# A two-layer hybrid decoder trunk: one eviction moved ahead of a softmax normalisation, the last round of transposes on four PSUM banks, the compressed values padded to 128 rows

## The reference

```python
def hybrid_layer(x, g, w_in, ...):
    h = rmsnorm(x, g)
    z = h @ w_in
    u_lru, g_lru, q, g_nsa, kc, vc, ks, vs, kwn, vwn, gate_logits = jnp.split(z, splits, axis=-1)
    y_lru = rg_lru(causal_depthwise_conv(u_lru, conv_w, conv_b), wa, ba, wi, bi, lam)
...
    o_cmp, p_cmp = cmp_attention(q, compress(heads(kc), pos_k, kw1, kw2), compress(heads(vc), pos_v, vw1, vw2))
...
    o_slc = slc_attention(q_rot, apply_rope(heads(ks), cos, sin), heads(vs), idx, ok)
    o_win = win_attention(q_rot, apply_rope(heads(kwn), cos, sin), heads(vwn))
    gates = jax.nn.sigmoid(gate_logits.astype(F32)).reshape(B, S, N_HEADS, 3)
    y_nsa = (gates[..., 0:1] * o_cmp + gates[..., 1:2] * o_slc + gates[..., 2:3] * o_win).reshape(B, S, D_NSA)
    y = jnp.concatenate([y_lru * jax.nn.silu(g_lru), y_nsa * jax.nn.silu(g_nsa)], axis=-1)
    return x + y @ w_out
```

## Time and profile before

| | |
|---|---|
| median of 3 runs | 543.06 us |
| the runs | 539.6, 543.06, 544.32 us |
| time of the profiled execution | 540.08 us |
| its span in the profile | 538.3 us |
| PE busy | 523.8 us, 97% |
| DVE busy | 379.9 us, 71% |
| ACT busy | 309.9 us, 58% |
| mean share of the DMA engines | 40 slices between 1 and 9 tenths, 102 GB/s |

### The profile page before, as it was taken

One profiled execution on the slowest core, in us unless ns is written; L12 is line 12 of the kernel. 1 busy time (PEld: TensorE's weight loads), 2 busy tenths in 40 slices (PEclk: granted clock), 3 DMA queues, 4 the chain that ended last, 5 costly groups with the idle time before them and its releaser, 6 DMA issues.

```text
span 538.3 us, 8590 instructions
## 1 busy us (share of the span) xinstructions
PE 523.8 (97%) x3095; PEld 395.6 (73%) x3095; DVE 379.9 (71%) x620; ACT 309.9 (58%) x625; POOL 46.8 (9%) x88
## 2 busy tenths in 40 slices
PE   8999999999899999999999999999989999999995
PEld 7777868778677766767887687678777777676784
DVE  3596996679857686855747589668986768678432
ACT  5757735624766666663534772653475656667523
POOL 4101100130000000000520110012100000000000
PEclk9999999999999999999999999999999999999999
DMA  9876464365222222321323845635523232111013
GB/s 263 203 226 185 97 180 103 73 149 126 76 74 65 56 55 69 79 58 40 90 90 98 213 124 142 119 94 119 136 62 96 61 97 52 50 38 34 8 41 117
DMA packets 102426, 54.65 MB, mean 102 GB/s; under 512 B 42080, under 2 KB 100592, under 8 KB 102384
## 3 DMA queue, kind: packets, MB, share of 16 engines
q1 hardware_dynamic: 99232, 49.63, 36.1%
q0 software_dynamic: 1536, 3.15, 2.4%
q10 hardware_dynamic: 1616, 1.32, 0.8%
HBM read 44.12 MB, written 2.10 MB: 86 GB/s over the span
## 4 chain that ended last, share of the span: by engine, by line
PE 67%; DVE 16%; issue 5%; SPq 4%; ACT 3%; DMA 3%; POOL 1%; POOLq 0%; DVEq 0%; ACTq 0%
PE z_ps L1634 10%; PE z_ps L1636 10%; PE z_ps L1635 10%; PE o_ps L1775 5%; PE t_ps L1737 5%; PE a_ps L1775 4%; PE s_ps L1714 3%; DVE w_lo L1233 3%; PE z_ps L1714 3%; PE o_ps L1634 3%; PE o_ps L1636 2%; PE o_ps L1635 2%; ACT probs L1160 2%; DMA swp<-E 2%; DVE E L1282 2%
## 5 line engine op out<-in xcount | busy, mean ns | idle before, releaser
L1634 PE MATMUL z_ps<-h_hi,w_hi 128*128 128x512 f32 x248 | 101.5, 409 | 4.3 <-DVE E L1282 4.2
L1636 PE MATMUL z_ps<-h_hi,w_lo 128*128 128x512 f32 x248 | 97.0, 391 | 0.0
L1635 PE MATMUL z_ps<-h_lo,w_hi 128*128 128x512 f32 x248 | 96.8, 390 | 0.0
L982 ACT ACTIVATE w_hi<-stage 128x1024 fp32r<-128x1024 f32 x54 | 57.1, 1058 | 53.9 <-PE z_ps L1636 29.1
L1233 DVE TENSOR_TENSOR w_lo<-stage,w_hi 128x1024 fp32r<-128x1024 f32 x54 | 65.9, 1220 | 8.6 <-ACT w_hi L982 7.9
L1169 ACT ACTIVATE probsT<-t_ps 128x512 f32<-128x512 f32 (+1 forms) x70 | 41.7, 595 | 43.8 <-PE t_ps L1737 34.1
L1634 PEld LDWEIGHTS z_ps<-h_hi,w_hi 128*128 128x128 f32 x248 | 46.6, 188 | 18.7 <-issue 8.2
L1636 PEld LDWEIGHTS z_ps<-h_hi,w_lo 128*128 128x128 f32 x248 | 46.5, 188 | 10.3
L1635 PEld LDWEIGHTS z_ps<-h_lo,w_hi 128*128 128x128 f32 x248 | 46.7, 188 | 8.3 <-issue 0.2
L1522 DVE TENSOR_REDUCE mn<-s_ps 128x1 f32<-128x384 f32 (+3 forms) x44 | 26.2, 637 | 32.4 <-PE s_ps L1722 32.3
L1160 ACT ACTIVATE probs<-s_ps,mn 128x128 f32<-128x128 f32 (+3 forms) x64 | 33.1, 527 | 16.4 <-DVE mn L1522 16.2
(11 more groups left out here) (266 smaller groups left out, 1052.7 us busy)
## 6 DMA issues: line engine op xcount, KB each, us to landing
stage<-in_w_in SPq DMA_DIRECT2D x27, 512.0 KB, 4.1
stage<-in_w_in SPq DMA_DIRECT2D x34, 256.0 KB, 3.9
probsT<-swp SPq DMA_DIRECT2D x72, 64.0 KB, 2.1
stage<-in_cmp_k_w SPq DMA_DIRECT2D x8, 512.0 KB, 4.0
stage<-in_cmp_v_w SPq DMA_DIRECT2D x8, 512.0 KB, 4.5
stage<-in_w_out SPq DMA_DIRECT2D x8, 512.0 KB, 3.3
stage<-in_w_out SPq DMA_DIRECT2D x16, 256.0 KB, 3.7
swp<-E POOLq DMA_DIRECT2D x48, 64.0 KB, 2.3
```

What stands on the lines that cost most here:

```text
L982: act.activation(split_into(n)[0], stage_of(key), ACT.Copy).then_inc(hi_split, 1)
L1634: pe.matmul(bank, w_hi[:, slot, at:at + P], x_hi, start=first, stop=False)
L1635: pe.matmul(bank, w_hi[:, slot, at:at + P], x_lo, start=False, stop=False)
L1636: ins = pe.matmul(bank, w_lo[:, slot, at:at + P], x_hi, start=False, stop=last)
```

## The change

In `attention`, the whole normalisation (now one step `CS2`) moves behind `close()`: DVE evicts gn0 first, and the multiply follows the four small instructions at once. On ACT the order of these steps is unchanged.

The coefficient turn ("B", 3, 1) moves from the end of round 11 to the end of round 12. Since the pieces of a round are spread over its turns, the four pieces of round 11 in layer 1 now stand two and two, and the four of round 12 one behind each turn. The tiles of round 12 use four banks, t_ps1 being the fourth; a turn on it waits for all exponentials of the layer.

vc_sb gets 128 rows, of which POOL zeroes all once at the start of the program, and the compressed tiles are weighed with all 128 rows. ACT still copies 31 rows of a turned compressed tile; the slot's other rows hold what an earlier tile left there and meet zeros.

```diff
@@ attention
     fill(N_START - 2)
-    add(("CS2", 0))
     close()
     split("HI")
-    add(("CS2", 1), *tanhs, *silus)
+    add(*tanhs, ("CS2",), *silus)
     split("LO")
...
-        if n in (1, 2, len(SETS) - 1):
+        if n == len(SETS) - 1:
+            owed, coefs = coefs, []
+        if n == len(SETS):
+            turns += owed
+        if n in (1, 2):
             turns += coefs
             coefs = []
@@ Plan
-            self.turn_bank.append(place[0] % 3 if place else 0)
+            self.turn_bank.append(place[0] if place else 0)
@@ hybrid_trunk
-        kc_bd, vc_sb = sb("kc_bd", [P, N_KV * NC]), sb("vc_sb", [NC, N_KV, HD])
+        kc_bd, vc_sb = sb("kc_bd", [P, N_KV * NC]), sb("vc_sb", [P, N_KV, HD])
...
-        score_banks, turn_banks = [s_ps, [z_ps[1], t_ps[1]]], [t_ps[0], *s_ps]
+        score_banks, turn_banks = [s_ps, [z_ps[1], t_ps[1]]], [t_ps[0], *s_ps, t_ps[1]]
...
-        N_CONST = 7
+        N_CONST = 8
...
-                eng.wait_ge(exp_ok, plan.exps[per_layer(plan.steps, plan.turns[n][0] + 1) - 1])
+                eng.wait_ge(exp_ok, plan.exps[per_layer(plan.steps, plan.turns[n][0] + 1) - (plan.turn_bank[n] < 3)])
...
+            pool.memset(vc_sb[:, :, :], 0.0).then_inc(consts, 1)
...
                 elif kind == "CS2":
-                    _, l, last = st
-                    if last:
-                        dve.tensor_tensor(sc3, sc3, spread(rsc), ALU.mult).then_inc(cs_ok, 1)
-                        continue
+                    l = st[1]
                     dve.wait_ge(cs_exp, l + 1)
...
+                    dve.tensor_tensor(sc3, sc3, spread(rsc), ALU.mult).then_inc(cs_ok, 1)
@@ weigh
                 for g in range(N_KV):
-                    if b < 2:
-                        v, rows = v_sb[:, b, k, g * HD:(g + 1) * HD], P
-                    else:
-                        v, rows = vc_sb[:, g, :], NC
+                    v = v_sb[:, b, k, g * HD:(g + 1) * HD] if b < 2 else vc_sb[:, g, :]
...
-                        turned = slot_of(key)[0:rows, g * 2 * P:(g + 1) * 2 * P]
+                        turned = slot_of(key)[:, g * 2 * P:(g + 1) * 2 * P]
```

More of the change, by code:

```diff
@@ L854, in _ @@
                 kind = st[0]
-                if st == ("CS2", DEPTH - 1, 0):
+                if st == ("CS2", DEPTH - 1):
                     sync.wait_ge(rot_ok, len(plan.rope))
@@ L1461, in _ @@
                     else:
-                        dve.tensor_scalar(vc_sb[:, :, :], bank[0:NC, 0:P].rearrange("p (g d) -> p g d", g=N_KV), 0.5, None,
+                        dve.tensor_scalar(vc_sb[0:NC, :, :], bank[0:NC, 0:P].rearrange("p (g d) -> p g d", g=N_KV), 0.5, None,
                                           ALU.mult).then_inc(a_dve, 1)
```

## The result

| | before | after |
|---|---|---|
| median of 4 runs | 543.35 us (539.6 to 544.32) | 535.08 us (534.57 to 535.71) |
| a second series | 540.98 us (11 runs, 539.94 to 543.22) | 534.64 us (4 runs, 534.44 to 535.18) |
| the profiled execution | 540.08 us, span 538.3 | 534.57 us, span 532.8 |

The ratio is 0.9882, with an interval from 0.9853 to 0.991; in the second series it is 0.9876, from 0.9856 to 0.9896. The changed kernel is 1.2% faster. The two profiled executions stand 5.5 us apart, near the sum of 5.1. But the series stand 6 to 8 us apart in their medians, and the runs of the changed kernel lie within about 1 us where those of before lie within 3 to 5. That is the first sign of something that the prediction left out.

The account below looks back on a forecast made before the run. PE's stream was taken to bound the kernel, busy for 523.8 of 538.3 us. Gains of 3.36 + 0.58 + 1.15 = 5.1 us took the median from 543.06 to 538.0 us, range 534.2 to 541.3.

Parts of the forecast that it names:

- The eviction: Gate chunk gn0, both layers: evicting before the normalisation restarts PE 1.68 us sooner per layer, 0.44 stays idle; gain 3.36 us.
- the copy's margin: ACT's copy of the first turned tile frees t_ps0 before PE's next turn, with 0.15 us less a release to spare.
- the release: Delay of some 0.07 us, taken off the 0.15 us by which ACT's copy precedes PE's next turn behind gn0.
- The padding: Rounds 5 to 8, eight places: compressed values with 128 rows avoid 0.14 to 0.15 us of pause each; gain 1.15 us.
- The rival that the tensor and not the form makes the pause: Padding gives nothing or costs (0.12): pause from changing tensor, or slower 128-row form; 0.06 over 32 pairs loses 1.8 us.
- The last round: Layer 0, rounds 11 and 12: moving the coefficient turn brings the second weighing from 241.85 to 241.27; gain 0.58 us.
- the landing: Round 11, layer 0: the first tile's last DMA transfer lands at 237.0 to 237.1, wanted at 237.05; costs 0 to 0.1.
- neighbours take a part back: Rival (0.12): ACT's copy or round 11's DMA is late, up to 0.8 per layer and 0.6; gain 3.0 to 4.6.
- the fourth bank: Round 12, layer 0: a fourth turn need not wait for the first one's copy; about 0.04 us of the 0.58.
- The sum: Whole kernel: 3.36 + 0.58 + 1.15 = 5.1 us gained, profiled execution 540.08 to 535.0, median 543.06 to 538.0.
- the stretch from 537.7 to 538.4: Median time in us if the forecast itself holds, with a gain of 4.7 to 5.4; chance 0.71.
- the likeliest case: Whole kernel's measured side: within 1% 0.57, faster 0.40, slower 0.03; 1% is 5.4 us, the sum 0.94%.

## Why the prediction was right, and where not

**The eviction** held in every step. PE restarted 1.67 and 1.68 us sooner, 0.44 of idle time stayed in each layer, the next turn kept its distance of 1.47, and the copy's margin, worked out as 0.15, was 0.18. But it was a closer thing than the prediction has it. It allowed 0.07 us for the release, a figure for which it names no row, and its own rows have 0.14 from the end of DVE's eviction to PE. With 0.14 the forecast left 0.01 us and the measured stream 0.04, so that this step held was in part luck. The late normalisation cost nothing that the waits show.

**The padding** held: 0.15 us at each of eight places, and the pairs of 128 rows run as those of v_sb do. The rival that the tensor and not the form makes the pause fell with the runs of 64 and 96 rows.

**The last round** had the right mechanism and a wrong size: 0.44 to 0.46 instead of 0.58. The term that failed is the landing, taken as 0 within a stated 0 to 0.1. It took 0.15, outside these bounds, because the weighing could start only at 234.59 and was wanted at 234.44. The rival "neighbours take a part back" showed itself there, well below the size given to it. (Two sums of the rivals are slightly off, without effect on the forecast: 5.1 less 0.8 twice and 0.6 is 2.9, not 3.0, and 32 pairs at 0.06 are 1.9, not 1.8.) A second term was read wrongly, though it did not move the sum: the fourth bank was given 0.04 us, the gain from a fourth turn without a wait. In the new order the coefficient turn stands right behind that turn and would share its bank. Without the fourth bank it loses 1.0 us. The bank's worth came from the other half of the same edit, and only one half was priced at a time.

**The sum** of 5.1 us is 5.0 in the aligned streams. The forecast of 535.0 for the profiled execution met 534.57. On the median 538.0 met 535.08. That lies inside the range from 534.2 to 541.3 only because the range starts from the fastest run of before; the stretch from 537.7 to 538.4, to which the prediction gave 0.71, was missed by 2.6 us.

**The side** was missed, at odds that were close: the likeliest case was within 1%, and it is 1.2% faster. The step that failed is the one from the profiled execution to the median. The prediction saw that the median lay 3.0 us above the profiled execution, subtracted 5.1 from both and did not ask what the 3.0 were. The experiments show it: granted-clock falls behind PE's 2.1 us of idle time. The idle time is 2.12 us per layer in the trace and cost, on average over 69 runs, 1.15 more in lost clock over both layers. Seven profiles of kernels with an idle time of 0.44 us at the gate chunks, and the one with the idle time filled, show no fall behind them. With 5.0 to 5.1 from the waits and pauses and 1.15 from the clock, 6.2 us or 1.15% is what the sum should have been; the second series gave 541.29 - 534.72 = 6.6 in the means, its 541.29 being that of all 69 runs. Without falls on either side it is 540.14 - 534.72 = 5.4, so 0.3 to 0.4 us have no account. The first series had a slower set of the kernel before (three of four runs over 543), and its 8 us are not typical.

The profile of before couldn't show the fall itself, since it had none. Three things that the prediction had could have raised the question: runs that spread over 4.7 us in a program on one core, a profiled execution at the lower end of them, and two idle times of 2.1 us in a PE that is otherwise busy for 97% of the span.

## What to carry to other kernels

Where PE is nearly always busy, price a wait of two microseconds or more with the clock that it may cost afterwards, and ask of a spread between runs what the slower ones do that the profiled one doesn't; the mean granted clock of each run sorts them, and gains that a median hides appear at equal clock. When an order is changed, follow each bank to its next user after the change: a bank that looked idle may be what makes the new place free of a wait, and a moved piece takes the eviction of its chunk with it. Where a narrow point is known to within 0.1 us, put the middle of its bounds in the sum, not its best end; here even the far end, 0.1, was passed by 0.05.

## What the runs showed of the hardware

- Behind 2.1 us of idle time of an otherwise busy PE the granted clock fell to 1.2 GHz in some executions and not in others. It fell at 3 of the 8 gate-chunk waits in four profiles (before, its repetition, the last round alone, the padding alone), and at both waits of 3.2 us. A third place, with an idle 2.25 us, had one in one of two profiles when a moved piece made PE wait there. None fell behind the 0.44 us at the gate chunks (seven profiles), nor behind the 0.9 to 1.1 us that PE waits at about 340 us in seven profiles. The falls began between 0.2 us ahead of PE's restart and 0.9 us behind it, and one cost 1.58 us where it was measured between two executions with the same instructions. The Trainium skill, TensorE: Matmul & The Clock Gate, Part 1, names these two states and says that the number of slow matmuls at a kernel's start varies from run to run. The spacings of 0.43 and 0.23 us agree with the two states, and that falls in the middle of one program come and go from run to run is what the groups of mean clocks show here. The page names a third state too, for three and more busy cores of a die, which no run here can show.
- A fall is hard to see. In the page of the repeated run every slice of the clock reads 9, and its mean is 0.995; the windows row and the distance between matmuls show it.
- Unused transposes in the idle time hold the clock: with 17 of them ahead of each gate chunk all 12 runs had a mean clock of 0.997 or 0.998.
- Going over from 128 rows to 64 or 31 on PE took 0.10 us more ahead of the change and about 0.05 at the way back; 96 rows took none.
